# A kernel of two transformer blocks on one core: roots of four norms taken on 128x2, Sqrt's table loaded earlier, two roundings set behind the norm

## The reference

```
y = x * rsqrt(mean(x * x, over the 2048 channels) + 1e-6) * g
x1 = x + g1 * rms_norm(merge(branches) @ w_o)            # norm y1
h  = rms_norm(x1) * (1 + sc2) + sh2                      # norm x1
x2 = x1 + g2 * rms_norm(relu(h @ up)**2 @ down)          # norm y2
h  = rms_norm(x2) * (1 + sc) + sh ; x3 = x2 + ga * mixer(h)      # norm x2
h  = rms_norm(x3) * (1 + sc) + sh                        # norm x3
out = rms_norm(x3 + gf * (silu(conv(h @ wg)) * (h @ wu)) @ wd)   # norm x4
```

## Time and profile before

| what | value |
|---|---|
| timed executions, us | 3455.66 (median), 3454.62, 3462.45 |
| profiled execution: its own time, us | 3459.0 |
| profiled execution: span, us | 3457.3 |
| mean granted clock of TensorE, of full speed | 0.984 |
| instructions | 57768 |
| HBM traffic | 203 GB/s over the span |

### The profile page before, as it was taken

One profiled execution on the slowest core, in us unless ns is written; L12 is line 12 of the kernel. 1 busy time (PEld: TensorE's weight loads), 2 busy tenths in 40 slices (PEclk: granted clock), 3 DMA queues, 4 the chain that ended last, 5 costly groups with the idle time before them and its releaser, 6 DMA issues.

```text
span 3457.3 us, 57768 instructions
## 1 busy us (share of the span) xinstructions
PE 3283.2 (95%) x23026; PEld 2687.1 (78%) x23026; DVE 2166.8 (63%) x3283; ACT 1183.7 (34%) x1550; POOL 188.6 (5%) x298
## 2 busy tenths in 40 slices
PE   6899989989998899998999999998999999999998
PEld 3674676457777799987888888886888788888887
DVE  2185654663333565667777777787656767667767
ACT  1212021022222321234434343444544543444344
POOL 0000000111222100000000000000000000000000
PEclk9999999999999999999999999999999999999999
DMA  9864624722112477754676767673444556656654
GB/s 364 327 230 170 264 105 158 292 92 84 71 44 84 190 309 307 292 185 158 246 263 235 272 229 282 231 268 122 158 153 176 172 193 234 235 187 229 233 177 151
DMA packets 99280, 706.33 MB, mean 204 GB/s; under 512 B 11008, under 2 KB 11008, under 8 KB 17920
## 3 DMA queue, kind: packets, MB, share of 16 engines
q1 hardware_dynamic: 74880, 523.27, 41.5%
q0 software_dynamic: 23184, 169.88, 13.3%
q10 hardware_dynamic: 1008, 10.23, 0.7%
HBM read 697.05 MB, written 6.29 MB: 203 GB/s over the span
## 4 chain that ended last, share of the span: by engine, by line
PE 76%; DVE 9%; issue 6%; ACT 4%; DMA 3%; DVEq 0%; ACTq 0%; SPq 0%; POOLq 0%
PE ps L2352 25%; PE ps L2351 13%; PE ps L535 10%; PE ps L966 6%; PE ps L2086 3%; ACT rows_parts L2310 3%; PE ps L355 2%; PE ps L1542 2%; PE ps L2348 2%; PE ps L2068 2%; PE ps L2067 2%; PE ps L2069 2%; PE ps L1556 1%; DVE work L2196 1%; DMA ring<-in_conv_u 1%
## 5 line engine op out<-in xcount | busy, mean ns | idle before, releaser
L2352 PE MATMUL ps<-hT_parts,rows_parts 128*128 128x512 f32 x3210 | 1129.8, 394 | 0.0
L2351 PE MATMUL ps<-hT_parts,ring_parts 128*128 128x256 f32 x3210 | 900.7, 281 | 2.0 <-DVE hT_parts L2324 2.0
L2315 DVE TENSOR_TENSOR ring_parts<-ring,rows_parts 128x2048 fp32r<-128x2048 f32 (+1 forms) x340 | 769.6, 2264 | 208.6 <-ACT rows_parts L2310 207.2
L2310 ACT ACTIVATE rows_parts<-ring 128x2048 fp32r<-128x2048 f32 (+1 forms) x340 | 643.8, 1895 | 414.9 <-DMA ring<-in_mlp_u 167.6
L2352 PEld LDWEIGHTS ps<-hT_parts,rows_parts 128*128 128x128 f32 x3210 | 603.5, 188 | 125.6
L2351 PEld LDWEIGHTS ps<-hT_parts,ring_parts 128*128 128x128 f32 x3210 | 608.0, 189 | 12.9 <-DVE hT_parts L2324 3.2
L2352 PE MATMUL ps<-work_parts,rows_parts 128*128 128x512 f32 x1616 | 573.3, 396 | 0.0
L2351 PE MATMUL ps<-work_parts,ring_parts 128*128 128x256 f32 x1616 | 453.1, 280 | 4.6 <-DVE work_parts L2540 4.6
L535 PE MATMUL ps<-hT,ring 128*128 128x512 f32 (+1 forms) x1088 | 374.2, 505 | 7.4 <-ACT work L1294 4.3
L2352 PEld LDWEIGHTS ps<-work_parts,rows_parts 128*128 128x128 f32 x1616 | 303.6, 188 | 68.2
L535 PEld LDWEIGHTS ps<-hT,ring 128*128 128x128 f32 x1088 | 206.0, 190 | 173.8 <-issue 162.1
(11 more groups left out here) (444 smaller groups left out, 3784.3 us busy)
## 6 DMA issues: line engine op xcount, KB each, us to landing
ring<-in_mlp_u SPq DMA_DIRECT2D x128, 1024.0 KB, 4.9
ring<-in_ffn_u SPq DMA_DIRECT2D x88, 1024.0 KB, 4.8
rows<-in_mod_r POOLq DMA_DIRECT2D x64, 1024.0 KB, 5.2
ring<-in_gate_u SPq DMA_DIRECT2D x64, 1024.0 KB, 6.7
work<-in_ada_r POOLq DMA_DIRECT2D x64, 1024.0 KB, 5.1
ring<-in_in_u SPq DMA_DIRECT2D x36, 1024.0 KB, 4.8
ring<-in_mod_u SPq DMA_DIRECT2D x32, 1024.0 KB, 7.7
rows<-in_ada_r POOLq DMA_DIRECT2D x32, 1024.0 KB, 7.6
```

Of the source, the lines that this page charges most:

```text
L2310: act.activation(unit_high(u)[:, 0:size], slot(u)[:, 0:size], ACT.Copy).then_inc(hi_done, 1)
L2315: dve.tensor_tensor(ring_parts[:, u % SLOTS, 0:size], slot(u)[:, 0:size], unit_high(u)[:, 0:size].bitcast(F32), ALU.subtract)\
L2351: pe.matmul(ps[:, b, low_half], low, top(kt), start=False, stop=False)
L2352: mm = pe.matmul(ps[:, b, :], high, both(kt), start=False, stop=kt == kts - 1)
```

## The change

Each summed norm gets a second use of a PSUM bank. TensorE makes the sum as two products with `sq_sum` as the stationary side and one column of ones as the moving side, so that the tokens come to lie on the partitions: 128x2 in place of 128x256. Sqrt and reciprocal work on these two columns, in a new tile `root`. Two more products, a column of `root` broadcast to 128x128 as the stationary side and the identity as the moving side, spread the root into rows again, in the second bank, and VectorE's multiplications of that norm read the rows from there (`rms.rows`); a norm that isn't summed keeps `rtn`. VectorE frees the bank behind its last multiplication. For the share of GpSimd the last norm is spread a second time, into `use_last`, and ScalarE copies this into `rtn` for it.

A tiny Sqrt (`load_root`) is put at the start of ScalarE's part of Mix, at the start of its part of Ffn2, and ahead of the last down projection. The loops of Mix and of Ffn2's output projection run three rounds, the fourth is written out, and its last rounding comes behind the norm's Sqrt. Below, the lines that pass the norm to `add_scaled` and `scale_split`, and `use_last = aux()` beside the norm x4, are left out.

```diff
@@ -186,6 +186,7 @@
         rows4, w_high = sb_and_parts("rows4", [P, SLOTS, UNIT])
         rows_buf, c_row = rows4[:, 0:G_SLOTS, :], rows4[:, G_SLOTS:, :]
         g_acc = sb("g_acc", [P, G_SLOTS])
+        root = sb("root", [P, TT + 1])
         csT = sb("csT", [P, KT, 2])
         modT = sb("modT", [P, 32, 2])
         modx = sb("modx", [P, 64])
...
@@ -2227,6 +2228,10 @@
                     sums_added[0] += summed + reset
                     self.total = sums_added[0]
                 self.use = aux()
+                self.rows = rtn
+                if summed:
+                    self.spread = aux()
+                    self.rows = ps[:, self.spread[0], 0:T]
 
             def square_out(self, act, src, dst):
 
...
@@ -2247,15 +2252,26 @@
 
             def tensor(self, pe):
                 acquire(pe, self.use)
-                if self.summed:
-                    pe.wait_ge(sq_added, self.total)
-                    pe.matmul(ps[:, self.use[0], 0:T], kc("ones"), sq_sum, start=True, stop=True).then_inc(bk.full[self.use[0]], 1)
+                if not self.summed:
+                    for kt in range(KT):
+                        if kt % self.step == 0:
+                            pe.wait_ge(nsq, self.first + kt // self.step + 1)
+                        mm = pe.matmul(ps[:, self.use[0], 0:T], kc("ones"), self.squares[:, kt, :], start=kt == 0, stop=kt == KT - 1)
+                    mm.then_inc(bk.full[self.use[0]], 1)
                     return
-                for kt in range(KT):
-                    if kt % self.step == 0:
-                        pe.wait_ge(nsq, self.first + kt // self.step + 1)
-                    mm = pe.matmul(ps[:, self.use[0], 0:T], kc("ones"), self.squares[:, kt, :], start=kt == 0, stop=kt == KT - 1)
+                pe.wait_ge(sq_added, self.total)
+                for a in range(TT):
+                    mm = pe.matmul(ps[:, self.use[0], a:a + 1], sq_sum[:, a * P:(a + 1) * P], kc("ones", 0, 1), start=a == 0, stop=a == TT - 1)
                 mm.then_inc(bk.full[self.use[0]], 1)
+                acquire(pe, self.spread)
+                pe.wait_ge(nrs, self.k)
+                self.spread_root(pe, self.spread)
+
+            def spread_root(self, pe, use):
+
+                for a in range(TT):
+                    mm = pe.matmul(ps[:, use[0], a * P:(a + 1) * P], root[:, a:a + 1].to_broadcast([P, P]), kc("ident"), start=True, stop=True)
+                mm.then_inc(bk.full[use[0]], 1)
 
             def scalar(self, act):
                 if not self.summed:
...
@@ -2264,34 +2280,49 @@
                         both = slice(2 * n, 2 * n + 2)
                         act.activation(self.squares[:, both, :], self.src[:, both, :], ACT.Square).then_inc(nsq, 1)
                 full(act, self.use)
-                emptied(self.use, act.activation(rtn, ps[:, self.use[0], 0:T], ACT.Sqrt, bias=eps(EPS_RMS), scale=1.0 / D))
+                to, n = (root[:, 0:TT], TT) if self.summed else (rtn, T)
+                emptied(self.use, act.activation(to, ps[:, self.use[0], 0:n], ACT.Sqrt, bias=eps(EPS_RMS), scale=1.0 / D))
 
             def vector(self, dve):
                 evacuated(dve, self.use)
-                dve.reciprocal(rtn, rtn).then_inc(nrs, 1)
-                dve.wait_ge(nrs, self.k)
-
-        def add_scaled(dve, own, src, col):
+                to = root[:, 0:TT] if self.summed else rtn
+                dve.reciprocal(to, to).then_inc(nrs, 1)
+                if self.summed:
+                    full(dve, self.spread)
+                else:
+                    dve.wait_ge(nrs, self.k)
+
+            def read(self, eng):
+                if self.summed:
+                    eng.sem_inc(bk.free[self.spread[0]], 1)
+
+        def load_root(act):
+
+            act.activation(root[:, TT:TT + 1], eps(ONE), ACT.Sqrt)
+
+        def add_scaled(dve, own, src, col, rms):
 
             for kt in range(KT + 1):
                 if kt < KT:
-                    own.step(dve.tensor_tensor(src[:, kt, :], src[:, kt, :], rtn, ALU.mult))
+                    own.step(dve.tensor_tensor(src[:, kt, :], src[:, kt, :], rms.rows, ALU.mult))
                 if kt:
                     own.settle(1 if kt < KT else 0)
                     t = kt - 1
                     dve.scalar_tensor_tensor(xT[:, t, :], src[:, t, :], col[:, t:t + 1], xT[:, t, :], ALU.mult, ALU.add).then_inc(nadd, 1)
-
-        def scale_split(dve, k, col, shift):
+            rms.read(dve)
+
+        def scale_split(dve, k, col, shift, rms):
 
             lag = 2
             for n in range(KT + lag):
                 if n < KT:
-                    dve.scalar_tensor_tensor(hT[:, n, 0:T], xT[:, n, :], col[:, n:n + 1], rtn, ALU.mult, ALU.mult).then_inc(hsc, 1)
+                    dve.scalar_tensor_tensor(hT[:, n, 0:T], xT[:, n, :], col[:, n:n + 1], rms.rows, ALU.mult, ALU.mult).then_inc(hsc, 1)
                 if n >= lag:
                     t = n - lag
                     dve.wait_ge(hrd, k * KT + t + 1)
                     dve.scalar_tensor_tensor(h_low[:, t, :], hT[:, t, 0:T], shift[:, t:t + 1], h_high[:, t, :].bitcast(F32), ALU.add, ALU.subtract)\
                         .then_inc(x_split, 1)
+            rms.read(dve)
 
         def shift_round(act, k, shift):
             for kt in range(KT):
...
@@ -2425,13 +2456,21 @@
                 rms_x1.tensor(pe)
 
             def scalar(act, own):
-                with act.Fori(0, KT // 4) as it:
+                load_root(act)
+                def wo_out(it, last=False):
+
                     for j in range(4):
                         small_out(act, seg_wo + j, j % 2, yT1[:, bass.ds(it * 4 + j, 1), :], SECOND, wo_half, it * 4)
                         act.wait_ge(bk.free[j % 2], it * 2 + (use_wo[j % 2][1] + j // 2 + 1))
                         rms_y1.square_out(act, yT1[:, bass.ds(it * 4 + j, 1), :], sq1[:, bass.ds(it * 4 + j, 1), :])
-                        round_unit(act, seg_wo + j + AHEAD_ACT, it * 4)
+                        if not last or j < 3:
+                            round_unit(act, seg_wo + j + AHEAD_ACT, it * 4)
+
+                with act.Fori(0, KT // 4 - 1) as it:
+                    wo_out(it)
+                wo_out(KT // 4 - 1, last=True)
                 rms_y1.scalar(act)
+                round_unit(act, seg_wo + KT - 1 + AHEAD_ACT)
                 rms_x1.scalar(act)
                 shift_round(act, 0, modx[:, KT:2 * KT])
 
...
@@ -3131,15 +3171,25 @@
                             unit_products(pe, seg_dn[n] + j, (j % 2, use_dn[n][j % 2][1] + j // 2), low_then_high(act_parts), it * 4, it, 2, kts=tiles,
                                           ready=hidden_ready if j == 0 else None)
                 rms_x4.tensor(pe)
+                acquire(pe, use_last)
+                rms_x4.spread_root(pe, use_last)
 
             def scalar(act, own):
-                with act.Fori(0, KT // 4) as it:
+                load_root(act)
+                def out2_out(it, last=False):
+
                     for j in range(4):
                         small_out(act, seg_out2 + j, j % 2, y3[:, bass.ds(it * 4 + j, 1), :], SECOND, out2_half, it * 4)
-                        round_unit(act, seg_out2 + j + AHEAD_ACT, it * 4)
+                        if not last or j < 3:
+                            round_unit(act, seg_out2 + j + AHEAD_ACT, it * 4)
                         act.wait_ge(nadd, it * 4 + (2 * KT + j + 1))
                         rms_x3.square_out(act, xT[:, bass.ds(it * 4 + j, 1), :], squared[:, j % 2:j % 2 + 1, :])
+
+                with act.Fori(0, KT // 4 - 1) as it:
+                    out2_out(it)
+                out2_out(KT // 4 - 1, last=True)
                 rms_x3.scalar(act)
+                round_unit(act, seg_out2 + KT - 1 + AHEAD_ACT)
                 shift_round(act, 2, adaT[:, 3 * KT:4 * KT])
                 act.wait_ge(gpad_zero, 1)
                 first = 0
...
@@ -3168,6 +3218,8 @@
                     act.wait_ge(gmul, first + tiles)
                     act.activation(act_high[:, tiles - 1:tiles, :], gcv[:, 1:2, :], ACT.Copy).then_inc(ghi, 1)
                     last = n + 1 == len(PARTS2)
+                    if last:
+                        load_root(act)
 
                     def square_scale(it, j):
 
...
@@ -3187,6 +3239,8 @@
                             square_scale(KT // 4 - 1, j)
                     first += tiles
                 rms_x4.scalar(act)
+                full(act, use_last)
+                act.activation(rtn, ps[:, use_last[0], 0:T], ACT.Copy).then_inc(nrs, 1)
 
             def gpsimd(pool, own):
                 pool.wait_ge(nadd, 3 * KT)
...
@@ -3194,7 +3248,7 @@
                 pool.memset(gpad.rearrange("p r t -> p (r t)"), 0.0).then_inc(gpad_zero, 1)
                 pool.wait_ge(x_split, 4 * KT + 1)
                 fetch_late(pool, LATE_ROWS, GATE_ROWS)
-                pool.wait_ge(nrs, rms_x4.k)
+                pool.wait_ge(nrs, rms_x4.k + 1)
```

(5 more changed lines are left out.)

8 lines of the change are left out of this document (3 added, 5 removed).

## The result

Over five runs each the kernel after took 3437.99 us (median, 3436.59 to 3442.86) and the kernel before 3455.66: a ratio of 0.9946, 95% interval 0.9932 to 0.9960. The medians lie 17.7 us apart and the ratio puts the gain at 0.54%, where 7.3 us were forecast. The range began at 3443.5.

The account below looks back on a forecast made before the run. TensorE, busy 3283.2 of 3457.3 us, was taken as the bound, with gains only where it stands still: 2.78 + 0.61 + 1.25 + 1.56 + 1.11 = 7.31 us, against the median 3455.66 giving 3448.3, range 3443.5 to 3454.5.

Parts of the forecast that it names:

- x4: Last of the four summed norms, ahead of the output: from VectorE's last addition to the multiplications 1.56 us shorter.
- The chain at the norms: From VectorE's last addition through sum, Sqrt, reciprocal and spread to its first multiplication: 2.05 us, each product step 0.59.
- what is put at nothing: Costs taken as zero: PSUM reads, moved table loads, second spread, added waits, the kept bank, peeled loop rounds.
- y1: First of the four summed norms, ahead of the MLP: 4.83 us less the new chain's 2.05, a gain of 2.78.
- nothing in y1 and x4: Charge for TensorE's clock falling before the spread: none at these two norms, 0.3 us in x3, 0.25 in y2.
- if a spread takes over 1 us: Named sign of a wrong forecast: the products spreading the root, put at 0.59 us, lasting over 1 us.
- y2: Second summed norm, where VectorE reaches the reciprocal no earlier: 0.86 us less 0.25 for the clock, a gain of 0.61.
- x3: Third summed norm: square 0.44 us earlier, then the 2.05 us chain plus 0.3 for the clock, a gain of 1.25.
- The rival of a low clock: Sums and spreads all at 1.2 GHz, about 0.4 us more for each of 8: gain only 4.7 us, chance 0.12.
- the clock staying up: Rival: shorter gaps behind the norms keep the clock at 1.00 until the next products; gain 8 to 10.5 us, chance 0.14.
- The output: Behind x4: GpSimd starts later, so VectorE's first output part runs alone and the end comes 1.11 us earlier.
- its second reason: In the output, VectorE's second input is now in PSUM, so GpSimd does not hold its multiplications later either.

## Why the prediction was wrong

The chain at the norms was right, with its spreads priced too low, and the sum missed two mechanisms outside it.

- **What failed**: the list of what is put at nothing. It asks what each addition costs on its own engine and for none where it moves the instructions behind it; "Peeling the last round of two loops adds a few ScalarE instructions" is all it says on their number. It names the bank that VectorE keeps, but not the signal that frees it, one instruction more ahead of the MLP. That signal moved a loop that had stalled 7 us at each back edge: 11.4 us. The wait of 20.4 us for issue at L2400 stood in the trace before; I had read the waits of TensorE alone.
- **What was missed beside it**: the new tile `root` moved `work`, and five small tiles, by 32 bytes: 5.0 us. No row of the kernel before could have shown that.
- **The norms**: 5.78 us for 7.31. y1 gave 2.24 for 2.78 and x4 0.94 for 1.56, because the spread took 1.19 us in y1 and 1.26 in x4 (from 3431.64 to 0.04 ahead of the multiplication). Windows of TensorE in the kernel after:

```profile
1581.00:1581.50 0.50, 0.36 (x4) 0.78 1.16 492
...
2325.00:2325.50 0.50, 0.49 (x4) 0.89 1.00 426
...
3431.00:3431.50 0.50, 0.00 (x0) 0.81 0.00 0
```

  I had put nothing for the clock in y1 and x4, since in x4 it was still 1.00 at 3446.5. In the kernel after it fell in these half microseconds, 0.4 to 0.9 us behind the start of the sums at 1580.79, 2325.01 and 3430.42 (1.00 until the fall and 0.50 behind it give the shares shown). That it held there before was one execution's luck. With the old norms it fell 2.7 us behind x4's last addition in the kernel before, 1.1 behind it with one instruction more, and 0.3 ahead of it with 257 more (granted clock of 0.64 in 3431.50:3432.00 and of 0.91 in 3438.50:3439.00, the additions at 3430.50 and 3439.18). With the new norms, where it held through the spread, y1 took 2.09 us for the 2.05 of the sum. So the step that failed here is "nothing in y1 and x4", read off one execution; what decides when it falls stays open. A sign of being wrong was named, "if a spread takes over 1 us", and it came. y2 gave 0.24 for 0.61 for the same reason, and x3 1.32 for 1.25. The rival of a low clock was half right: sums ran at full speed (0.57 to 0.64 for 0.59), spreads didn't. Its price came from eight products of 128x2 at 40.42, in a stretch for which the trace of the kernel before has no clock; in the kernel after the same eight take 1.83 us, at a granted clock of 0.50.
- **Sqrt and reciprocal** of 128x2 took 0.26 and 0.17 us for 0.30 and 0.15; no load stood at Sqrt. PSUM operands cost nothing (0.42 and 0.48 us a tile, as before).
- **The output** gained 1.04 for 1.11. GpSimd did start later, 1.25 us behind VectorE, so that the first part ran alone, as was written. But by the run with GpSimd later that only moves the hold to another part; the gain is the PSUM operand's, which the prediction gave as its second reason.
- **The chances**: a gain beyond 0.3% had 0.12, put down to the clock staying up and to low runs; it came from none of the rivals.

## What to carry to other kernels

Look at the waits for issue of every engine, not of the busiest alone. A long loop (here 322 instructions) can be one instruction away from a stall at each back edge, so a change ahead of it should be compared with a twin that has the same shift; likewise a new small tile moves all tiles behind it. When the granted clock falls differs from one execution to the next, so what it takes from a short chain is read from several profiles. An edit's own part is read from the stage that it touches, never from the total.

## What had not been expected of the hardware

- VectorE's loop of 322 instructions stalled at its three back edges at two positions (20.4 and 22.7 us in all at 1985, 12.9 at 2185) and not at all at three others.
- Products of 128x512 whose moving operand begins 96 bytes above a multiple of 128 took 573 to 575 us per 1616, at the other three places 565 to 570, and M was 5.0 to 9.6 us longer than at 0.
- Beside GpSimd's product a VectorE product with two SBUF inputs took 2.29 to 2.32 us for 1.22, and with one of them in PSUM no longer; GpSimd's took 1.26 us beside one of the held ones and 2.17 beside the other.
- The same norms in six profiles took 2.09 to 2.60 us at y1 and 2.15 to 3.07 at x4, by whether TensorE's clock fell to 1.2 GHz ahead of the spread or behind it; with ten small products beside them the spreads ran at 2.4 GHz in all three kernels, and it was 1.96 and 2.03 us each time.
